# A two-layer decoder trunk on one core: expert coefficients from two small zero strips instead of a 16 KB diagonal buffer, and two weight pieces that stay in that buffer

## What is computed

```python
for l in range(2):
    mod = silu(c) @ w_ada[l] + b_ada[l]                    # 6 vectors of 1024
    h = rms_norm(x) * (1 + sc1) + sh1
    q, k, v, qi, ki, wi, cu = split(h @ w_in[l])
    attn = sparse_attention(...)                           # a scored choice of keys
    conv = conformer_conv(cu, ...)                         # 31 taps, LayerNorm, silu
    x = x + g1 * (concat(rms(attn), rms(conv)) @ w_out[l])
    h2 = rms_norm(x) * (1 + sc2) + sh2
    # PEER: per token 8 heads x 16 experts chosen out of 16384
    coef = softmax(top_s) * gelu(dot(u[e], h2))            # 128 per token
    x = x + g2 * sum_j coef[j] * v[e_j]
```

## Time and profile before

| | us |
|---|---|
| runs before | 1896.24, 1879.58, 1887.08; median 1887.08 |
| span of the profiled execution (first to last instruction) | 1733.4 |
| median less span (what lies around the instructions) | 153.7 |

### The profile page before, as it was taken

How to read it: one execution, slowest core, us unless ns; L and a number is a source line. 1 busy time by engine, 2 the same in 40 slices (tenths; PEclk the granted TensorE clock), 3 DMA queues, 4 the chain that set the end, 5 groups by cost and what they waited for, 6 DMA issues and landing times.

```text
span 1733.4 us, 18207 instructions
## 1 busy us (share of the span) xinstructions
PE 1039.2 (60%) x6158; PEld 590.6 (34%) x6158; DVE 1103.2 (64%) x3003; ACT 273.4 (16%) x717; POOL 1015.9 (59%) x1133
## 2 busy tenths in 40 slices
PE   7979897406896588603788569611689610005555
PEld 4547674303363156301345146500236200001111
DVE  1987989996218576888117676889513979991000
ACT  2141235202110035300101024400210100000000
POOL 2610435676655763566755664567655777776774
PEclk8989899657998799655899679765899865557888
DMA  9998999999999999999999999999999999999998
GB/s 373 393 368 327 405 405 383 409 409 409 409 409 407 408 404 410 397 410 397 410 409 409 394 409 408 399 407 409 406 406 402 391 410 410 409 410 389 409 409 330
DMA packets 195481, 691.98 MB, mean 399 GB/s; under 512 B 21360, under 2 KB 21376, under 8 KB 195134
## 3 DMA queue, kind: packets, MB, share of 16 engines
q0 software_dynamic: 147840, 537.06, 78.1%
q1 hardware_dynamic: 47550, 153.77, 22.8%
HBM read 689.71 MB, written 1.05 MB: 398 GB/s over the span
## 4 chain that ended last, share of the span: by engine, by line
DMA 41%; PE 24%; DVE 15%; POOL 13%; issue 6%; ACT 1%; SPq 0%; DVEq 0%; ACTq 0%; POOLq 0%
DMA rows<-in_peer_v,v_at 20%; DMA rows<-in_peer_u,u_at 18%; PE ps L921 8%; DVE rows L1586 8%; PE ps L876 7%; POOL rows L698 7%; POOL rows L690 6%; DMA kiw<-in_w_in 1%; PE ps L818 1%; PE ps L864 1%; PE ps L848 1%; DMA rows<-in_w_ada 1%; DVE rows L1568 1%; PE ps L735 1%; PE ps L804 1%
## 5 line engine op out<-in xcount | busy, mean ns | idle before, releaser
L690 POOL DMA_INDIRECT rows<-in_peer_u,u_at x512 | 482.5, 942 | 370.8 <-DVE dots L1586 202.5
L1586 DVE CUSTOM_DVE_ANT_0 rows<-rows,ps 128x1024 f32<-128x1024 f32 x512 | 610.3, 1219 | 92.5 <-DMA rows<-in_peer_u,u_at 78.6
L698 POOL DMA_INDIRECT rows<-in_peer_v,v_at x512 | 485.7, 949 | 283.9 <-PE ps L921 153.4
L921 PE MATMUL ps<-rows,spread_c 128*32 128x512 f32 x2048 | 325.7, 764 | 215.0 <-DMA rows<-in_peer_v,v_at 215.0
L735 PE MATMUL ps<-ident 128*128 128x128 f32 x228 | 39.9, 346 | 354.3 <-DVE dots L1586 354.3
L921 PEld LDWEIGHTS ps<-rows,spread_c 128*32 128x32 f32 x2048 | 71.4, 125 | 414.8 <-issue 412.6
L735 PEld LDWEIGHTS ps<-ident 128*128 128x128 f32 x228 | 35.6, 183 | 369.8 <-DVE dots L1586 356.6
L876 PEld LDWEIGHTS ps<-hT,wring 128*128 128x128 f32 x1152 | 137.0, 199 | 25.7 <-issue 24.1
L876 PE MATMUL ps<-hT,wring 128*128 128x128 f32 x1152 | 142.2, 285 | 0.0
L848 PE MATMUL ps<-wring,hT 128*128 128x512 f32 x256 | 117.1, 600 | 8.3 <-DMA wring<-in_w_in 7.5
L902 PE MATMUL ps<-diag_eq,hc 128*128 128x128 f32 x744 | 104.7, 307 | 25.3 <-ACT diag_eq L1274 25.2
(11 more groups left out here) (254 smaller groups left out, 1183.9 us busy)
## 6 DMA issues: line engine op xcount, KB each, us to landing
wring<-in_w_in SPq DMA_DIRECT2D x34, 1024.0 KB, 13.2
wring<-in_w_ada SPq DMA_DIRECT2D x31, 1024.0 KB, 10.6
wring<-in_peer_wq SPq DMA_DIRECT2D x28, 1024.0 KB, 9.6
rows<-in_w_ada SPq DMA_DIRECT2D x16, 1024.0 KB, 14.9
wring<-in_w_out SPq DMA_DIRECT2D x13, 1024.0 KB, 17.1
rows<-in_peer_u,u_at POOLq DMA_INDIRECT x512, 14.1
rows<-in_peer_v,v_at POOLq DMA_INDIRECT x512, 9.5
rows<-in_w_in SPq DMA_DIRECT2D x6, 1024.0 KB, 15.9
```

The costliest lines, as they stand in the source:

```text
L690: pool.indirect_dma_start(row(n), None, u_rows, bass.IndirectOffsetOnAxis(ap=u_at[:, p % 2, k:k + 1], axis=0)).then_inc(row_landed[n % SLO ...
L698: pool.indirect_dma_start(row(n), None, v_rows, bass.IndirectOffsetOnAxis(ap=v_at[:, p % 2, tok:tok + 1], axis=0)).then_inc(row_landed[n % ...
L921: ins = pe.matmul(ps[32 * g:32 * g + 32, YB + q, :], spread_c[:, g, a, :], row(n)[:, q * 512:q * 512 + 512], start=a == 0, stop=a == 31)
L1586: dve.tensor_tensor_reduce(out=row(n), in0=row(n), in1=h2_shown, scale=1.0, scalar=0.0, op0=ALU.mult, op1=ALU.add, accum_out=dots[:, k:k + ...
```

## The change

1. A buffer `window`, [128, 2, 4, 63], zero everywhere, with one column (31) for the coefficients of the current group. The 32 columns that start at 31 - a show the coefficient in column a. Two copies (a % 2) alternate. Parts 0, 1 and 2 use it; part 3 still uses spread_c.
2. For each group a from 2 on, POOL copies the 4 coefficients per partition into window (`put_window`), between its DMA issues: for a = 2 to 29 right after it has issued item 4a + 8, for a = 30 after all items and a wait for item 115's use, for a = 31 after the fifth u row of the next part. Groups 0 and 1 are written by VectorE. TensorE waits for the count of these copies before each group from 2 on.
3. VectorE leaves the transposed coefficients in `coef` for POOL.
4. spread_c is free through parts 0 to 2. Pieces 0 and 1 of "vqi" of part 2 are loaded into its halves and stay there for part 3, which no longer loads them. SP waits only for part 1's use of the kept "v" pieces before that load, not for a ring slot.
5. ScalarE's clearing of spread_c moves from the end of part 0 to the end of part 3's `second`.

```diff
+STAYED = {(("vqi", 3), h): (("vqi", 2), h) for h in range(2)}
-    uses = [(n, h) for n in blocks for h in range(pieces(n))]
+    uses = [(n, h) for n in blocks for h in range(pieces(n)) if (n, h) not in STAYED]
         if name == ("v", 0):
             slot = KEPT[h]
+        elif (name, h) in STAYED.values():
+            slot = KEPT[h]
+        window = sb("window", [P, 2, 4, 63])
@@
-                if use_before[i] is not None:
+                if (name, h) in STAYED.values():
+                    b, n = bank(("v", 1))
+                    sp.wait_ge(full[b], n)
+                elif use_before[i] is not None:
@@
+            seq_(pool.memset(window[:, :, :, :], 0.0))
+            def put_window(p, a):
+                if a == 2:
+                    pool.wait_ge(coef_turned, p + 1)
+                seq_(pool.tensor_copy(window[:, a % 2, :, 31], coef[:, a:P:32]), window_ready)
...
+                    if p and k == 4:
+                        put_window(p - 1, 31)
...
+                    if p + 1 < PARTS and m >= 16 and m % 4 == 0:
+                        put_window(p, m // 4 - 2)
+                if p + 1 < PARTS:
+                    pool.wait_ge(v_used, p * P + 116)
+                    put_window(p, 30)
@@
-                i = use_at[(name, h)]
+                i = use_at[STAYED.get((name, h), (name, h))]
-                    if h < 3:
+                    if (name, h) in piece_count:
@@
+                    if p + 1 < PARTS and a > 1:
+                        pe.wait_ge(window_ready, 30 * p + a - 1)
-                            ins = pe.matmul(ps[32 * g:32 * g + 32, YB + q, :], spread_c[:, g, a, :],
+                            c = window[:, a % 2, g, 31 - a:63 - a] if p + 1 < PARTS else spread_c[:, g, a, :]
+                            ins = pe.matmul(ps[32 * g:32 * g + 32, YB + q, :], c,
@@
-                if p == 0:
-                    wait_full(act, ("v", 1))
+                if p + 1 == PARTS:
+                    wait_full(act, ("qi", p))
                      act.copy(spread_c[:, :, :, :].rearrange("p g a c -> p (g a c)"),
                              hc[:, 0, 0:1].to_broadcast([P, 4096])).then_inc(spread_cleared, 1)
@@
-                if p:
-                    dve.wait_ge(v_used, p * P)
+                if p + 1 < PARTS:
+                    if p:
+                        dve.wait_ge(v_used, p * P)
+                    seq_(dve.tensor_copy(window[:, 0, :, 31], o[:, 0:P:32]))
+                    seq_(dve.tensor_copy(window[:, 1, :, 31], o[:, 1:P:32]), spread_ready)
+                    give(dve.tensor_copy(coef[:, :], o[:, 0:P]), name)
+                    dve.sem_inc(coef_turned, 1)
                 else:
                     dve.wait_ge(spread_cleared, 1)
...
```

More of the change, by code:

```diff
@@ L485, in trunk @@
         spread_cleared = sem("spread_cleared")
+        coef_turned = sem("coef_turned")
+        window_ready = sem("window_ready")
         x_done = sem("x_done")
@@ L1927, in coefficients @@
                 o = wait_full(dve, name)
-                if p:
-                    dve.wait_ge(v_used, p * P)
+                if p + 1 < PARTS:
[5 more added lines that the diff above has]
+                    dve.sem_inc(coef_turned, 1)
                 else:
                     dve.wait_ge(spread_cleared, 1)
-                diagonal = spread_c[:, :, :, :].rearrange("p g a c -> p g (a c)")[:, :, 0:1024:33]
-                give(dve.tensor_copy(diagonal, o[:, 0:P].rearrange("p (g a) -> p g a", g=4)), name)
-                dve.sem_inc(spread_ready, 1)
+                    diagonal = spread_c[:, :, :, :].rearrange("p g a c -> p g (a c)")[:, :, 0:1024:33]
+                    give(dve.tensor_copy(diagonal, o[:, 0:P].rearrange("p (g a) -> p g a", g=4)), name)
+                    dve.sem_inc(spread_ready, 1)
             first(0)
```

## The result

| kernel | median of its runs | before beside it | ratio, 95% interval |
|---|---|---|---|
| changed | 1906.44 (1898.38 to 1910.80, 7 runs) | 1887.76 | 1.0087 (1.0061 to 1.0113) |
| changed, once more | 1918.43 (10 runs) | 1904.29 | 1.0063 (1.0034 to 1.0093) |

The forecast was 1884 us, 3 us faster. By the two ratios the change costs some 12 to 16 us, where the forecast had a gain: inside "within 1%" but outside the range of 1874 to 1898. The median of the kernel before itself differs by 17 us between these two sets of runs, so each ratio is taken against the runs of before beside it; it isn't the exact quotient of the two medians.

A forecast was written before the change was run, and what follows sets the result against it. The prediction took the kernel to be bound by its DMA bytes. Two pieces less, -5.1 us, and POOL's copies, +2, with all else at 0, gave -3.1 us: 1887.1 to 1884.0 us, range 1874 to 1898.

The forecast's parts named there:

- within 1%: Whole kernel: claimed a time less than 18.9 us faster or slower than before, chance 0.91.

## What to carry to other kernels

Compare the profiled span with the timed median before anything else; where they differ by per cents, take another profile before adding microseconds. On an engine that issues DMAs into a ring of slots, keep small work whose end the engine waits for away from the place just ahead of the issue that waits for its slot, even though the engine is idle there, and put it behind that issue. When a helper adds a wait, look at what the next instruction then has to wait for. With several streams on the DMA engines, ask which one the chain waits for: slowing the other was a gain here, though why is not shown.

## What was not expected of the hardware

- An indirect DMA on GpSimd that waits for a slot starts 0.26 us after the release where it carries that wait itself (61 of 62 v issues before). Where the wait is an instruction of its own ahead of it, it starts 0.76 us after (39 of 48 in the changed kernel), behind a copy that ended 4 us earlier as well as behind another DMA with no copy at all.
- One kernel had one execution of 1733 us of span and otherwise 1873 us and more, with the same bytes and a mean granted clock of 0.792 against 0.756. In part 3's pure v rows the 1.24 us pace broke in the fast execution at each eighth row, by 0.3 us, and in every later profile at each sixteenth, by 3 us. The cause of the two kinds wasn't found.
- Idle instructions among the u issues made the kernel faster, by 1.0 to 1.1% with 90 and 2.3% with 180.
